# Encoder layer on one core: one written-out order for the recurrence's slabs, and another place for the mixture gates

## What is computed

```
proj = x @ w_in + b_in            # -> u_lru, g_lru (1280 each), q (1024), k, v (256 each), 2 mixture gates (1024 each)
u = depthwise_conv(u_lru)         # 4 taps over the positions
h = rg_lru_scan(u, forward) + flip(rg_lru_scan(flip(u), backward))
    # r, i = sigmoid(block_diag(u)) for each direction, 8 blocks of 160 channels
    # a = exp(8 r log_sigmoid(lam)); h[t] = a h[t-1] + sqrt(1 - a^2) (i u[t])
y_lru = (h * gelu(g_lru)) @ w_lru_out
y_attn = windowed_gqa(q, k, v) @ w_attn_out     # 8 heads, 2 kv heads, blocks of 128 queries, band of 384 keys
x = layer_norm(ALPHA x + (sigmoid(gate1) y_lru + sigmoid(gate2) y_attn) @ w_o)
y = layer_norm(ALPHA x + gated_mlp_with_conv(x))
```

## Time and profile before

| | us |
|---|---|
| median of 3 runs (3125.81 to 3128.97) | 3126.49 |
| the profiled execution's own time | 3127.93 |
| its span, first to last instruction | 3126.0 |
| PE busy | 2787.5 (89%) |
| PEld busy | 2278.2 (73%) |
| DVE busy | 1663.6 (53%) |
| POOL busy | 1188.7 (38%) |
| ACT busy | 784.2 (25%) |
| mean granted clock of TensorE, share of full speed | 0.939 |
| PE's share of the chain that ended last | 74% |

### The profile page before, as it was taken

How to read it: one execution, slowest core, us unless ns; L and a number is a source line. 1 busy time by engine, 2 the same in 40 slices (tenths; PEclk the granted TensorE clock), 3 DMA queues, 4 the chain that set the end, 5 groups by cost and what they waited for, 6 DMA issues and landing times.

```text
span 3126.0 us, 35166 instructions
## 1 busy us (share of the span) xinstructions
PE 2787.5 (89%) x12056; PEld 2278.2 (73%) x12056; DVE 1663.6 (53%) x1749; ACT 784.2 (25%) x1064; POOL 1188.7 (38%) x660
## 2 busy tenths in 40 slices
PE   8968899899799969999999999586799797999996
PEld 5757778778688857888888888465577685777774
DVE  3886754434305145463544635687845343666666
ACT  3655622303200032010110111065522212111110
POOL 2433432121133312333233332464544364566662
PEclk9989999899899979999999999798899898999998
DMA  4232321222754221111111111332323653222221
GB/s 140 80 107 74 109 105 61 88 64 78 280 187 141 74 67 34 50 51 47 40 54 47 54 47 40 122 106 92 117 98 116 228 191 102 68 89 90 90 87 67
DMA packets 115544, 295.43 MB, mean 95 GB/s; under 512 B 11206, under 2 KB 38086, under 8 KB 115464
## 3 DMA queue, kind: packets, MB, share of 16 engines
q1 hardware_dynamic: 51904, 176.84, 17.4%
q10 hardware_dynamic: 63560, 117.56, 10.7%
HBM read 227.77 MB, written 55.57 MB: 91 GB/s over the span
## 4 chain that ended last, share of the span: by engine, by line
PE 74%; DVE 14%; ACT 5%; issue 3%; ACTq 2%; DMA 1%; POOL 1%; DVEq 0%; POOLq 0%
PE ps L580 47%; PE ps L849 13%; PE ps L720 5%; PE ps L635 3%; PE ps L749 2%; PE ps L703 2%; DVE tau L1329 1%; DVE g_conv L1526 1%; DVE small L1475 1%; DVE HH L1536 1%; PE ps L638 1%; DVE sig L1327 1%; DVE ln_out L1564 1%; DVE v_conv L1526 1%; ACTq L1114 1%
## 5 line engine op out<-in xcount | busy, mean ns | idle before, releaser
L505 POOL TENSOR_SCALAR w_head<-raw 128x1024 fp32r<-128x1024 f32 (+2 forms) x304 | 345.0, 1135 | 1836.7 <-PE ps L580 1187.1
L580 PE MATMUL ps<-XH,w_head 128*128 128x512 f32 x2400 | 819.0, 396 | 99.0 <-ACT u_raw L929 54.1
L580 PE MATMUL ps<-XL,w_head 128*128 128x512 f32 x2400 | 813.9, 393 | 0.0
L580 PE MATMUL ps<-XH,w_tail 128*128 128x512 f32 x2400 | 812.6, 393 | 0.0
L506 POOL TENSOR_TENSOR w_tail<-raw,w_head 128x1024 fp32r<-128x1024 f32 (+2 forms) x304 | 772.4, 2541 | 25.4
L580 PEld LDWEIGHTS ps<-XH,w_head 128*128 128x128 f32 x2400 | 457.7, 191 | 204.3 <-issue 58.7
L580 PEld LDWEIGHTS ps<-XL,w_head 128*128 128x128 f32 x2400 | 457.8, 191 | 96.3
L580 PEld LDWEIGHTS ps<-XH,w_tail 128*128 128x128 f32 x2400 | 456.7, 190 | 96.5
L849 PE MATMUL ps<-HH,w_head 128*128 128x512 f32 x576 | 198.9, 399 | 22.5 <-DVE HL L1537 22.5
L1544 DVE TENSOR_TENSOR acc<-ps,acc 128x1024 f32<-128x1024 f32 (+1 forms) x96 | 92.0, 958 | 201.7 <-PE ps L849 197.9
L849 PE MATMUL ps<-HL,w_head 128*128 128x512 f32 x576 | 197.4, 397 | 0.0
(11 more groups left out here) (182 smaller groups left out, 3534.8 us busy)
## 6 DMA issues: line engine op xcount, KB each, us to landing
raw<-w_mlp SPq DMA_DIRECT2D x144, 512.0 KB, 3.3
raw<-w_qkv_mix SPq DMA_DIRECT2D x56, 512.0 KB, 3.4
raw<-w_u SPq DMA_DIRECT2D x20, 512.0 KB, 3.5
raw<-w_g SPq DMA_DIRECT2D x20, 512.0 KB, 3.6
raw<-w_lru SPq DMA_DIRECT2D x16, 640.0 KB, 4.8
gate_dram<-mix_out ACTq DMA_DIRECT2D x16, 512.0 KB, 2.7
gate_in<-gate_dram ACTq DMA_DIRECT2D x16, 512.0 KB, 4.4
raw<-w_attn SPq DMA_DIRECT2D x16, 512.0 KB, 3.2
```

The source lines that it names most:

```text
L505: order(pool.tensor_scalar(w_head[slot][:, 0:width], raw[raw_slot][:, 0:width], 1.0, 1.0, ALU.mult, ALU.mult))
L580: last = nc.tensor.matmul(bank(group, c), lhs(wl, k), rhs(xl, k, c), start=(k == 0 and n == 0), stop=(k == nk - 1 and n == 2))
```

## The change

The two halves of the recurrence are no longer a loop. One order of 28 slabs is written out, with the second half's first channels between gate products of the first half and each gelu rest tile between two gate products of its half; the same order holds for both sequences. The projected u now always comes ahead of g between two gate products. ACT takes what lies between two gate products always behind the roots; the rests' channels of the second half are convolved and split by DVE inside the first half's rests' tile. A tile's tau buffer now follows its number in the whole, not in its half.

For attention the four slabs at the end of the recurrence are the first four q slabs instead of mixture gates; two mixture gates (LEAD) follow k and v of the first kv head in PSUM groups 2 and 3, and the blocks hold 8 (first kv head) and 6 (second) instead of 6 and 6. No arithmetic, slab, tile or evacuation is added or dropped.

```diff
 EARLY = 4
-FILL = (16 - EARLY) // KV
+LEAD = 2
+FILLS = (8, 6)
+MIX_AT = (LEAD, LEAD + FILLS[0])
...
+        order_lru = [("u", 0, REST_TILE), ("u", 0, 0), ("u", 0, 1),
+                     ("gates", 0, 0), ("u", 0, 2), ("g", 0, 0), ("g", 0, REST_TILE),
+                     ("gates", 0, 1), ("u", 0, 3), ("g", 0, 1),
+                     ("gates", 0, 2), ("u", 1, 0), ("g", 0, 2),
+                     ("gates", 0, 3), ("g", 0, 3), ("u", 1, REST_TILE), ("u", 1, 1),
+                     ("gates", 1, 0), ("u", 1, 2), ("g", 1, 0),
+                     ("gates", 1, 1), ("u", 1, 3), ("g", 1, 1),
+                     ("gates", 1, 2), ("g", 1, 2), ("g", 1, REST_TILE),
+                     ("gates", 1, 3), ("g", 1, 3)]
@@ ACT @@
+                    take("u", 0, REST_TILE)
+                    take("u", 0, 0)
+                    stack_rests(act, q, T, 0, 0)
+                    take("u", 0, 1)
+                    for h in range(2):
                         for jj in range(HALF):
...
+                            decays(h, jj, [side(r, jj, T) for r in sig[0:2]])
                             if jj == HALF - 1:
+                                store_y(act, q, T, h, jj - 1)
+                            if h and jj == 0:
+                                store_y(act, q, T, 0, REST_TILE)
+                            roots(h, jj)
+                            if jj < HALF - 1:
+                                for e in behind_gates(h, jj):
+                                    take(*e)
+                        take("g", h, HALF - 1)
                         act.wait_ge(rest_moved[q], 64 * (HALF * h + HALF + 1))
+                        decays(h, REST_TILE, [r[:, 0:T] for r in sigr[0:2]])
+                        if h == 0:
+                            take("u", 1, REST_TILE)
+                        roots(h, REST_TILE)
+                        store_y(act, q, T, h, HALF - 1)
+                        if h == 0:
+                            take("u", 1, 1)
+                            stack_rests(act, q, T, 1, 0)
@@ DVE @@
+                            decay_steps(h, jj, r_i[0:2], r_i[2:4], u[jj % 2])
+                            recur(h, jj, r_i[0:2], r_i[2:4], side(gelu_g, jj, T))
+                            if jj < HALF - 1 and blk + 2 < BLOCKS:
+                                convolve((blk + 2) // HALF, (blk + 2) % HALF)
                         dve.wait_ge(rest_moved[q], 64 * (HALF * h + HALF + 1))
                         r_i = [z[:, 0:T] for z in sigr]
+                        decay_steps(h, REST_TILE, r_i[0:2], r_i[2:4], ur)
+                        if h == 0:
+                            convolve(1, REST_TILE)
+                            split_channels(1, REST_TILE)
+                        recur(h, REST_TILE, r_i[0:2], r_i[2:4], gelu_gr[:, 0:T])
+                        if h == 0:
+                            convolve(1, 1)
@@ PE, attention @@
-                        for n in range(6):
+                        for n in range(EARLY if kv == 0 else 0, 6):
...
+                        if kv == 0:
+                            for m in range(LEAD):
+                                pe.wait_ge(qkv_evac[q], 2 + m + 1)
+                                project(2 + m, T, s0 + 6 + m, m % 2)
```

More of the change, by code:

```diff
@@ L659, in _ @@
+                    for e in order_lru[AHEAD if q else 0:]:
+                        if e[0] == "gates":
+                            gates(e[1], e[2])
+                        elif e == order_lru[0]:
+                            proj(e, lambda k: pe.wait_ge(x_split, KD * q + k + 1))
+                        else:
+                            proj(e)
                     for m in range(EARLY):
@@ new lines, in take_gelu, with take @@
+                    def take_gelu(h, jj):
+                        last = 5 * (h - 1) + HALF if jj == REST_TILE else side_user(h, jj, T)
+                        if last is not None and last >= 0:
+                            act.wait_ge(y_ready[q], last + 2)
+                        take_projection(("g", h, jj), gelu_gr[:, 0:T] if jj == REST_TILE else side(gelu_g, jj, T),
+                                        ACT.Gelu_apprx_tanh, col("b_g", feature_tile(h, jj)))
+                    def take(kind, h, jj):
+                        take_channels(h, jj) if kind == "u" else take_gelu(h, jj)
@@ new lines, in decays @@
+                    def decays(h, jj, r):
+                        n, tile = 5 * h + jj, feature_tile(h, jj)
+                        for d in range(2):
+                            act.wait_ge(y_stored[q], 32 * n)
+                            A1(tau[n % 2][d][:, 0:T], r[d], ACT.Tanh, scale=decay_n[:, bass.ds(d * RT + tile, 1)]).then_inc(decay_done[q], 1)
+                        for d in range(2):
+                            act.wait_ge(decay_done[q], 6 * n + d + 1)
+                            A1(r[d], r[d], ACT.Exp, scale=decay_p[:, bass.ds(d * RT + tile, 1)]).then_inc(decay_done[q], 1)
+                        for d in range(2):
+                            act.wait_ge(decay_done[q], 6 * n + d + 3)
+                            if d and jj < REST_TILE and not is_short(T):
+                                act.wait_ge(rest_moved[q], 64 * (HALF * h + jj + 2))
+                            A1(square(d, T), r[d], ACT.Square).then_inc(decay_done[q], 1)
@@ new lines, in roots @@
+                    def roots(h, jj):
+                        n = 5 * h + jj
+                        for d in range(2):
+                            act.wait_ge(q_ready[q], 2 * n + d + 1)
+                            A1(tau[n % 2][d][:, 0:T], tau[n % 2][d][:, 0:T], ACT.Sqrt).then_inc(root_done[q], 1)
+                    take("u", 0, REST_TILE)
[3 more added lines that the diff above has]
+                    for h in range(2):
@@ L1070, in fills @@
                         def fills(n):
-                            return [EARLY + FILL * kv + f for f in range(n * per_block, min(FILL, (n + 1) * per_block))]
+                            return [MIX_AT[kv] + f for f in range(n * per_block, min(FILLS[kv], (n + 1) * per_block))]
                         def heads_of(n):
@@ new lines, in convolve @@
+                    def convolve(h, jj):
+                        number, tile = channel_at[(h, jj)], feature_tile(h, jj)
+                        dst = ur if jj == REST_TILE else u[jj % 2]
+                        dve.wait_ge(conv_begun[q], number + 1)
+                        for k in range(1, 4):
+                            ins = V.scalar_tensor_tensor(out=dst[:, 0:T], in0=u_raw[:, k:k + T], scalar=col("conv_w", RT * k + tile),
+                                                         in1=dst[:, 0:T], op0=ALU.mult, op1=ALU.add)
+                            if k < 3:
+                                order(ins)
+                            else:
+                                tell(ins, raw_read[q], number + 1)
```

389 lines of the change are left out of this document (151 added, 238 removed).

## The result

The changed kernel took 3052.65 us (median of 4 runs, 3050.38 to 3056.0) beside 3127.07 for the kernel before in the same session: ratio 0.9762, 95% interval 0.9745 to 0.9779, so 74.4 us less. Its profiled execution took 3053.1 us, span 3051.2 (before: 3127.9 and 3126.0).

What follows compares the result with a forecast made beforehand. PE was taken to bound the kernel, busy 2787.5 of 3126.0 us. Terms of 23.0, 15.8, 16.0 and 6.4 summed to 61.2 us off 3127.9; the median lies 1.4 lower: 3065, inner range 3051 to 3077, full range 3043 to 3090.

Steps and rivals of the forecast that it cites:

- 1. long, up to G3: Long recurrence to the end of the first half's last gate product: +2.1 us, a second slab ahead of block 3.
- 2. long, crossing: Long sequence, between the recurrence's halves: -27.7 us; PE waits 17.3 us for the rests' stack instead of 21.6.
- 3. long, second half: Long recurrence's second half, from its first gate product to its last: 108.8 us before, 111.4 after, +2.6 us.
- 4. short: to G3, crossing, half, tail: Short recurrence, -15.8 us in all: crossing wait 17 us, three blocks per half winning about 2 us each.
- 5. attention: Attention: ten slabs ahead of the first kv head's blocks become eight, unfilled blocks filled: -16.0 us long, -6.4 short.
- rival (a): Recurrence: DVE becomes the bound; twelve ordinary long blocks each 2 us longer, 3089 us; chance 0.25 together with (c).
- (b): Crossing of the halves: stack's wait near the short end, 11 us less at each of two crossings, 3043; chance 0.12.
- (c): Crossing of the halves keeps its price: waits of 27 and 22 us instead of 17, 3080; chance 0.25 with rival (a).
- (d): Recurrence: late gelu holds DVE in each of 16 blocks, slower than before, 3142 us; chance 0.05 with anything like it.
- The 3082 worked out with (a): Long crossing: if DVE and POOL fully block each other, its chain takes in POOL's work on three slabs, 3082 us.
- (e): Attention: the fill doesn't hide, as the last block's softmax comes late, 3073 us; counted inside the forecast's 0.56.

Runs made afterwards that it cites:

- e4: Changed kernel with the convolution and split of the second half's rest channels behind the first half's rests' scans on DVE: 3074.69 us.
- e7: Changed kernel with the second half's rest channels convolved and split ahead of the rests' root arguments, stack DMAs issued ahead of the rests' roots: 3055.37 us.
- e9: Changed kernel with the rests' gate products ahead of block (0,3)'s scans, their convolution before its last four DVE operations, stack DMAs before rests' roots: 3050.53 us.
- e12: e9 with the rests' root arguments ahead of block (0,3)'s last DVE operations, ACT taking u(1,1) before the stack, y stored behind two sigmoids: 3059.57 us.
- e6: Changed kernel with ACT's roots behind the next channels and gelu in the short sequence's blocks, as in the kernel before: 3056.56 us.
- after: The changed kernel itself, against the kernel before: 3052.65 us, ratio 0.9762.
- e3: Changed kernel with gelu slabs projected ahead of the channels in the five gaps that hold both: 3056.80 us.
- e10: e9 with, in the short sequence, the next channels' convolution between a block's root arguments and its scans: 3050.39 us.
- e11: Changed kernel with POOL forming only 16 columns of each weight slab's tail in the short recurrence: 3028.39 us.

## Why the prediction was right, and where it was off

The time lies in the range and 12 us under the forecast, near the low end of the inner range (3051 to 3077); the sum said 61.2, the spans 74.8. By its parts, with the same landmarks (long G3 184.80 and 181.35, measured from the first matmul; short G3 2105.87 and 2057.25, from 2024.28 and 1971.46):

| term | predicted | measured |
|---|---|---|
| 1. long, up to G3 | +2.1 | -2.6 |
| 2. long, crossing | -27.7 (wait 17.3) | -29.3 (15.59) |
| 3. long, second half | +2.6 | -1.0 |
| 4. short: to G3, crossing, half, tail | +3.0, -16.2, -0.5, -2.1 | +4.2, -16.5, -1.2, -1.0 |
| 5. attention | -16.0, -6.4 | -18.8, -4.0 |
| not in the sum | 0 | -4.7 |

**Terms 1 and 3 were mis-sized, by 4.7 and 3.6 us; the mechanism held.** I kept the first product of the long sequence at about its old 13.1 us: before, its granted clock was 0.87, with a pair of matmuls at 1.05 us for 0.63 behind a wait of 1.85; after, it is 1.00 behind a wait of 1.25, in 11.0 us. I kept an ordinary block at 32.90; it is 32.63, as ACT begins the first sigmoid 4.0 us behind the product's start where it began 4.2 behind (PE's wait 1.15 for 1.51). And in the two gaps that end with two gelus in a row ACT needs no load for the last, so the products of (0,1) and (1,3) don't wait at all and take 9.7 us; term 3 had 11.1 for the last. The product behind the crossing's wait took 11.34 us, where I had put 12.7.

**Term 2 held for the reason given.** The wait ahead of block 4's product is the stack's, 15.59 where 17.3 was worked out; e4 shows that DVE's chain releases it. Its steps held one by one: DVE's last decay step ended 38.6 us behind G3 (38.5 in the sum), convolution and split 44.6, the stack was there at 48.4. What was too much is the 1.5 us for u(1,0), whose convolution and split DVE had done ahead of block (0,3). What the term didn't see is what lies behind the wait: e7, e9 and e12 shortened it, and in the long sequence gave nearly all of it back.

**Term 4 held in its sum, less so in its picture; that the sum fits so well is partly luck.** The blocks do win about 2 us on average, but by e6 the roots' move, which was to win it, is worth some 5 us in all six, under 1 each; no run isolates the rest. At the crossing PE waits 14.10 us for the stack and 2.38 for ACT's gelu ahead of the last slab, together 16.5 for the 17 of the sum. And the blocks win unevenly: from one product's start to the next 17.2 and 19.6 us for the 20.5 of the prediction, and then 8.7 us in one wait. That is rival (a) in the short sequence: DVE falls behind until ACT's roots wait for it (27.9 us in 10 waits, 21.4 of them at blocks; in the kernel before the roots of no block wait, only those of the rests' tiles). It had been weighed for the long blocks, where PE's work is just as long, and not for the short, where it is not: PE about 17 us a block (two slabs of 5.5 and a product), DVE and POOL 23.9.

**Term 5** erred by 2.8 and 2.4 in opposite directions. The filled blocks took 16.0 and 13.2 us at a clock of 1.00, as said (16.4 and 13.3). The rest fits the clock that the neighbours leave, which the sum didn't have: with the same attention and another recurrence ahead of it the nine variants e4 to e12 took 199.0 to 200.8 us for the short one at a mean granted clock of 0.94 to 0.95, where after took 202.8 and e3 202.5 at 0.92. In the nine the term is worth 6.0 to 7.8 us, and the 6.4 fits. So may the 4.7 us outside the edit come from the clock, but no run isolates them.

**Rivals.** (b) 11 us less at each crossing: refuted by the waits of 15.59 and 14.10. (c): refuted likewise. (d): DVE did wait for gelu in the long sequence, 6.9 us in 4 waits, but no long wait of PE or ACT there ended on its product. The 3082 worked out with (a) failed though the rule behind it holds: the landmark that POOL's work was added to, 220.15 + 3.17, had that work in it already (a step of 3.17 us for 1.23 of work), and the chain ended 48.4 us behind G3. (e): the fill hides. The reading that failed was the one used against (a): "30.80 and 16.97 busy us lie in 32.90" was taken as a sign that both engines work at once. An instruction's record grows while the other engine works (2.33 to 4.34 us), so busy times that overlap say nothing against blocking; only durations alone, set against those beside the other engine, tell.

## What to carry to other kernels

When a change takes one engine's waits away, add up the next engines' work in the same stretch at their durations *alone*, and add engines that block each other as if they were one: here that sum (235 us) said that the short recurrence, at 245.6 us, had little left to give (the change won 14.5). How much an order can still win is the time in which neither of the pair works: 16.4 us in after. The six further orders e6 to e10 and e12 left the pair at work for 214.6 to 219.1 us, and gave next to nothing. A wait that shrinks is a gain only when the landmark behind it moves too; read the restart, not the wait. And cost a moved slab with its clock: a gate product of the long sequence took 13.1, 11.3, 11.0 and 9.7 us by the waits at it and the level granted.

## What the runs showed of the hardware that I had not expected

DVE and POOL take turns at these instructions: one that began while the other engine's was under way ended its own duration alone, less 0.07 to 0.23 us, behind the other's end, in all 72 and 60 cases of after's short recurrence. So they traded busy time almost one for one: 45.2 us of DVE for 49.8 of POOL (e11 against after). Work that isn't edited can change by 3 us with what ran ahead of it: two unfilled attention blocks 25.0 us at a granted clock of 0.58 and 22.0 at 0.79. And a wait of 1.25 us left the long sequence's first product at a clock of 1.00, where one of 1.85 us in the kernel before went with 0.87.
